# Four 1 MB weight reloads issued as transfers of 120 and 8 partitions

## The reference

```python
def token_mixer(...):                      # attention heads beside gating heads
    ...
    merged = jnp.concatenate([rms_norm(attn, g_attn_out), rms_norm(sgu, g_gmlp_out)], axis=-1)
    return merged @ w_out, new_k, new_v, gv          # w_out: 1024 x 1024
...
xp = xp + mp                                         # token mixer
xp = xp + memory_attention(rms_norm(xp, g_cross[l]), mk, mv, w_cq[l], w_co[l])
xp = xp + peer_ffn(rms_norm(xp, g_ffn[l]), *peer_w)

def peer_ffn(xn, w_pq, sub_keys, u_tab, v_tab):      # 8 heads x 16 experts a token
    ...
    h = jnp.einsum('td,thkd->thk', xt, u_tab[idx])
    a = jax.nn.gelu(h) * gate
    return jnp.einsum('thk,thkd->td', a, v_tab[idx])
```

## Time and profile before

| | |
|---|---|
| Time, median of 3 runs | 1709.2 us (1706.84 to 1709.46) |
| Span of the profiled execution | 1705.7 us |
| DMA, mean over the span | 385 GB/s |
| TensorE (matmul) busy | 76% |
| VectorE busy | 68% |
| ScalarE busy | 47% |
| GpSimd busy | 38% |

### The profile page before, as it was taken

How to read it: one execution, slowest core, us unless ns; L and a number is a source line. 1 busy time by engine, 2 the same in 40 slices (tenths; PEclk the granted TensorE clock), 3 DMA queues, 4 the chain that set the end, 5 groups by cost and what they waited for, 6 DMA issues and landing times.

```text
span 1705.7 us, 21619 instructions
## 1 busy us (share of the span) xinstructions
PE 1297.6 (76%) x7069; PEld 474.5 (28%) x7069; DVE 1166.1 (68%) x2795; ACT 809.4 (47%) x2337; POOL 644.8 (38%) x584
## 2 busy tenths in 40 slices
PE   9999878887888777678777666777676766677765
PEld 4454523433444322123232111112111211111110
DVE  2444568887667677777777777777667677677764
ACT  1434366785444354455555454445444445444443
POOL 0000044443434344444444444444444344344441
PEclk9999989899999887879978888888889888877876
DMA  9434699999999999999999999999999999999995
GB/s 353 169 115 148 244 396 422 419 369 419 421 421 421 416 400 418 422 402 421 420 421 421 421 422 421 421 422 421 421 420 422 420 407 422 422 421 421 422 417 220
DMA packets 99041, 657.35 MB, mean 385 GB/s; under 512 B 12576, under 2 KB 17568, under 8 KB 22368
## 3 DMA queue, kind: packets, MB, share of 16 engines
q0 software_dynamic: 83056, 604.28, 85.7%
q1 hardware_dynamic: 15872, 51.68, 8.1%
HBM read 652.71 MB, written 4.19 MB: 385 GB/s over the span
## 4 chain that ended last, share of the span: by engine, by line
DMA 44%; PE 23%; DVE 12%; ACT 11%; issue 7%; POOL 1%; SPq 1%; ACTq 0%; DVEq 0%; POOLq 0%
DMA R<-in_peer_uv,R 42%; PE ps L2009 10%; PE ps L1543 4%; DVE R L1462 4%; PE ps L1802 3%; ACT L911 2%; ACT R L920 2%; PE ps L1515 2%; ACT R L915 1%; DMA R<-in_mem_prompt 1%; POOL R L641 1%; ACT L826 1%; ACT R L911 1%; DVE R L1285 1%; DVE R L1288 1%
## 5 line engine op out<-in xcount | busy, mean ns | idle before, releaser
L2009 PE MATMUL ps<-R 64*64 64x512 f32 x4528 | 729.8, 725 | 373.5 <-ACT R L920 373.3
L641 POOL DMA_INDIRECT R<-in_peer_uv,R x566 | 630.5, 1114 | 959.9 <-PE ps L2009 759.6
L1462 DVE CUSTOM_DVE_ANT_0 R<-R 128x1024 f32<-128x1024 f32 x566 | 688.3, 1225 | 383.2 <-DMA R<-in_peer_uv,R 376.5
L911 ACT ACTIVATE R<-R 128x1 f32<-128x1 f32 x576 | 115.8, 201 | 599.0 <-DVE R L1462 597.8
L2009 PEld LDWEIGHTS ps<-R 64*64 64x64 f32 x4528 | 134.2, 149 | 717.4 <-ACT R L920 638.0
L920 ACT ACTIVATE R<-R 128x64 f32<-128x64 f32 x576 | 200.3, 348 | 54.3 <-ACT R L915 1.5
L1802 PE MATMUL ps<-A,R 128*128 128x256 f32 (+1 forms) x640 | 220.7, 469 | 0.7 <-ACT R L802 0.7
L915 ACT ACTIVATE R<-R 128x1 f32<-128x1 f32 x576 | 169.8, 295 | 21.1 <-ACT R L911 0.4
L1802 PEld LDWEIGHTS ps<-A,R 128*128 128x128 f32 (+1 forms) x640 | 94.7, 198 | 259.4 <-issue 257.3
L1543 PE MATMUL ps<-A,R 128*128 128x512 f32 (+1 forms) x256 | 102.1, 551 | 0.0
L911 ACT ACT_TABLE_LOAD x60 | 77.0, 1283 | 9.1 <-DVE R L1462 8.1
(11 more groups left out here) (288 smaller groups left out, 937.5 us busy)
## 6 DMA issues: line engine op xcount, KB each, us to landing
R<-in_peer_uv,R POOLq DMA_INDIRECT x566, 16.9
A<-in_w_pq SPq DMA_DIRECT2D x8, 1024.0 KB, 10.6
A<-in_w_in SPq DMA_DIRECT2D x3, 2048.0 KB, 20.4
R<-in_w_out SPq DMA_DIRECT2D x5, 1024.0 KB, 9.1
x_res<-in_x_prompt SPq DMA_DIRECT2D x6, 512.0 KB, 9.3
R<-in_w_out SPq DMA_DIRECT2D x1, 3072.0 KB, 9.9
R<-in_x_promptT SPq DMA_DIRECT2D x4, 512.0 KB, 7.5
R<-in_w_cq SPq DMA_DIRECT2D x2, 1024.0 KB, 10.9
```

The costliest lines, as they stand in the source:

```text
L641: pool.indirect_dma_start(slots[slot_of[g]], None, I["peer_uv"][:, :], bass.IndirectOffsetOnAxis(ap=idx[:, b % 4, k:k + 1], axis=0)).then_ ...
L911: act.activation(hgelu[:, b % 2, col], hdot[:, b % 2, col], ACT.Gelu).then_inc(gelu_ready, 1)
L1462: dve.tensor_tensor_reduce(u, u, xn(t), 1.0, 0.0, ALU.mult, ALU.add, hdot[:, b % 2, k:k + 1]).then_inc(u_used, 1)
L2009: ins = pe.matmul(bank(2 * (t % 2) + q)[rows], diag[tokens, g % DIAGS, :], v_rows[slot_of[g]][tokens, c * 512:(c + 1) * 512], start=first, ...
```

## The change

Each of the four reloads is issued as two transfers: partitions 0 to 119, then partitions 120 to 127. Both add 16 to `ld_wout`, and TensorE waits for 32 a piece.

```diff
-                load(w_piece, out_src[:, q], ld_wout)
+                load(w_piece[:120], out_src[:120, q], ld_wout)
+                load(w_piece[120:], out_src[120:, q], ld_wout)
...
-                pe.wait_ge(ld_wout, 32 + 16 * (q + 1))
+                pe.wait_ge(ld_wout, 32 + 32 * (q + 1))
```

## The result

The changed kernel takes 1724.63 us (median of 5 runs, 1722.8 to 1726.61) against 1709.2 us (1706.84 to 1712.0), 1.009 of before with a 95% interval of 1.0077 to 1.0103. That is 15.4 us more (13 to 18 us by the interval), where 1709.5 us and no measurable change had been forecast, and it lies outside the range of 1705.0 to 1712.5 us.

What follows compares the result with a forecast made beforehand. The prediction took the sixteen full DMA engines to bound the kernel. Span 1705.7 + 0.3 us for the uneven rows, other terms 0, gives 1706.0; with 3.5 us around the span, 1709.5 us, range 1705.0 to 1712.5 us.

Steps and rivals of the forecast that it cites:

- The price of a row: In the reloads: one engine moves 26.2 GB/s, so a row of 8 KB takes 0.31 us; about +0.3 us over the sixteen engines.
- The same 4 MB: 0 us: In the four reloads: the same bytes are read, so 0 us for the sixteen engines taken together.
- How the rows are shared: In each reload: 120 rows go to 15 engines, 8 rows to eight; one engine 2.5 us less, eight 0.31 us more.
- rival D: In the reloads: rows are spread evenly whatever the shape, so the change does nothing; 1709.2 us, chance 0.08.
- rival C: In the reloads: the 120 rows go to eight engines, which do 10 us more and delay gathers; 1718.5 us, chance 0.09.
- Transfers that get in each other's way: Example of a slowdown by something not seen; no place or size given, chance 0.05.
- The sign of the landing: Landing of the 120-row transfers: near 9.5 us expected; 12 us or more would mean the rows go to eight engines.
- The point near 606 us: Where DMA engines run dry after the reloads: expected within 1 us of before; 8 to 10 us later if eight engines serve.
- SyncE's queue: On SyncE: four more issues of 0.33 us each, hidden in waits of tens of microseconds for TensorE; cost 0.
- TensorE's wait: At the fourth reload: weights land 0.3 to 1.0 us later, TensorE may stand still 0 to 0.5 us; cost 0.
- Rivals A and B: Spared engine is the lagging one: A, gain only until 606 us, 1707.7 us, 0.13; B, lead kept, 1705 us, 0.07.
- The rule of the Trainium skill that speaks against the change: For the reloads: transfers to disjoint partitions serialize on the same engines; nothing to win, extra issue hidden, sum +0.0 us.

## Why the prediction was wrong

**What bounds the kernel** was read rightly: DMA rate. One step behind it was wrong, and the rest followed.

**The price of a row failed.** "One engine moves 420 / 16 = 26.2 GB/s, so a row of 8 KB takes 0.31 us" was taken from transfers of 128 partitions and gathers of 128 partitions, the only kind in the earlier trace rows, and used for 120. The count of engines held and their speed did not: fifteen engines moved 214 GB/s, 14.3 GB/s each, 0.57 us a row. "The same 4 MB: 0 us" fell with it. The sum had +0.3 us where the trace has 18.0 us, 4.2 to 5.1 us for each of the four reloads. (By its own terms that +0.3 us is the low end: eight engines of sixteen at +0.5 to +1.25 us are a mean of 0.3 to 0.6 us. And the 3.5 us around the span are 1.8 us in every run on record; the rest is how far the profiled execution lay under the median. The time forecast is not changed by it.)

**How the rows are shared.** Fifteen engines was right (share 0.96, fifteen packets of 4 bytes a transfer), so the even sharing of rival D was wrong, and rival C with eight, at a share of 0.5, was wrong too, although its time of 1718.5 us came nearest. It is no credit: C's mechanism gives no loss for 112 and 16 or 64 and 64, and these lost 14 us each by their ratios.

**"Transfers that get in each other's way"** stood in the text with 0.05 and without a price. That was the case, and the trace of before could not have priced it. What could be asked of it is the bound: the edit's cost was bounded by counts of rows alone, and the rate at which a new shape moves is a second unknown. With half the rate as its lower end, 983,040 bytes at 210 GB/s take 4.7 us and not 2.5, four reloads add 9 us, and the range would have reached to at least 1718 us. That bound is still below the 1724.63 us measured.

**What would show each step.** "The DMA share should stay at 1.01" came true and meant nothing, since an engine that waits for the SBUF is as busy as one that moves. I should have named the GB/s beside it. The sign of the landing pointed to the wrong rival: where the 120 rows go alone, so that their landing can be read, it took 12.9 us in the median, and 12 us or more was to be C. The point near 606 us came 16 us later, more than the 8 to 10 us of rival C.

**SyncE's queue** was right: the issues took 0.30 to 0.35 us, and two transfers of 128 partitions cost nothing. **TensorE's wait** was sized too small: at the fourth reload it waited 1.06 us for the weights, over the 0 to 0.5 us forecast, since the piece landed late, by more than the 0.3 to 1.0 us of the prediction; in the earlier trace rows its first product came 10.3 us after the issue, now 14.3 us after 533.31 us:

```profile
547.62 3.72 PE L1516 MATMUL ps<-R 128*128 128x256 f32 x16 [1.06 <-DMA R<-in_w_out]
```

**Rivals A and B**, a gain from the spared engine: no run shows one. The tail is as long as before, so B is out. By the landings above, the late engine is among the eight that 8 rows use, so it *got* a row, and it is most likely not the one that 120 rows spare. That part of the forecast was right.

**The rule of the Trainium skill that speaks against the change** ("DMA: Bandwidth & Descriptors", "Rules for kernel authors": use one transfer of 128 partitions) had the right sign. By its reason, that both serialize on the same engines, I priced it at nothing; the measured price is 0.8% for 64 and 64. Its rule on the number of engines agreed with the share of 0.96 and the packets, fifteen and eight.

**Open.** How the rows of each shape are dealt to the engines was not seen, only that 120 neighbouring and 60 even partitions run at about half rate and 64 even ones nearer to full rate. That the reload and the gathers meet on the same paths is the reading that fits, and it is argued from the rates. And a split costs more beside the gathers than alone. An estimate from the rates measured alone, the parts of a reload one after the other: 120 and 8 rows take 983,040 / 214,000 + 65,536 / 61,000 = 5.7 us in place of 2.5, so 3.2 us more; 112 and 16 take 1.9 us more, 64 and 64 2.5 us, the 120 rows alone 2.3 us. Beside the gathers, by the rates from 400 to 600 us, these lost 4.5, 3.3, 4.2 and 3.8 us a reload. So the order of the splits is that of their own rates, and each has 1.3 to 1.7 us on top. The gathers' share of it is seen in the 18% above; why it is about the same for each I cannot say.

## What to carry to other kernels

Keep transfers into and out of the SBUF at all 128 partitions and cut them by columns; a cut by partitions can halve the rate of a transfer, and in a stream that fills the DMA engines it then slows the other transfers too. Only one cut by partitions was free here, 64 even and 64 odd ones, and it is not to be relied on: 60 even ones were slow. When DMA is the bound, read GB/s beside the busy share, and give a new transfer shape its own rate: a few transfers of it in an idle stretch at the kernel's end measure it.

## What the runs showed of the hardware

- Rates into the SBUF that fit sixteen paths of 26.6 GB/s: 426 GB/s with 128 partitions, 211 with 0 to 63, 209 with 0 to 31, 115 with 0 to 15. Two engines that write partitions 0 and 1 move 25 GB/s together.
- 120 neighbouring partitions 214 GB/s on fifteen engines, 112 284, 96 246, 64 even 381 and 334 in two runs, 60 even 235, 60 neighbouring 201.
- Out of the SBUF 419 GB/s with 128 partitions and 307 with 120; from memory to memory 367 and 355.
- Such a transfer slows other traffic: the gathers' time for a megabyte rose by 18% over 24 us.
- One DMA engine falls behind the others in the gathers: its landing comes 10 us after the median one near 1650 us.
